# Column-by-column stores from a side tile, and expert biases loaded in their final layout

## The chip, the cores and the metric

The kernel runs on one NeuronCore of one Trainium2 chip. The metric is the device time of one launch in microseconds (us), as the median of several runs. Five engines run their own instruction queues and meet at semaphores: TensorE (PE), VectorE (DVE), ScalarE (ACT), GpSimd (POOL) and SyncE (SP). SP does no arithmetic; it issues most of the transfers.

## The reference

One layer of a hybrid decoder for 256 prompt tokens and 8 sample tokens (264 columns in all). With `D` = 1024:

```
mod = silu(c) @ w_mod + b_mod                       # six rows of 1024: shift, scale, gate, twice
h   = rms_norm(x) * (1 + sc1) + sh1
p   = h @ w_in                                      # q | k | v | p_rw (1792 columns) | gate_a | gate_b
o_a = windowed attention (q, k, v, cache)
o_b, new_wkv = rwkv7_mix(p_rw, prev_row, wkv0, ...)
new_shift = p_rw[:, -1]                             # last token of each sequence, 1792 features
x   = x + gt1 * ((sigmoid(g_a) * (o_a @ w_pa) + sigmoid(g_b) * (o_b @ w_pb)) @ w_o)
y   = moe(rms_norm(x) ...)                          # top 4 of 32 experts
    expert e: u = xe @ w1[e] + b1[e];  clamped SwiGLU;  act @ w2[e] + b2[e]
```

Two pieces matter here. `new_shift` gives the outputs `shift_prompt` (1 row of 1792) and `shift_sample` (8 rows of 1792). `b1` is 32 experts by 2048 biases, 256 KB.

## The kernel before

All activations are kept transposed: features on the 128 partitions, the 264 tokens along the free dimension. The order of the work on every engine is written out by hand; there is no scheduler.

**Weights.** SP walks a list `stream` of 2 MB chunks (`mod` = 512 columns of `w_mod`, `win` = 512 columns of `w_in`, then `pa`, `pb`, `wo`) into six ring slots, and afterwards the experts' `w1` and `w2` in 2 MB pieces. Before each load it waits until the slot's last user is done (`chunk_used`, L332). All these loads go through SP's one queue in this order, so whatever is put between two of them delays the later one. `win` 5 is loaded when `win` 4 has been used, then two copies of the caches (L409, L410), then `win` 6; `mod` 9 follows when the four gate groups of `win` 5 are done.

**TensorE** projects `win` 0 to 4 into `PT` (the 20 blocks of 128 features up to the end of `p_rw`) with modulation chunks between them (L941, L972), then interleaves the gate columns (`gates`, L962) with attention and the recurrence, and needs `mod` 9 at L1143 (`modulation(9)`).

**The shift rows.** `p_rw` of the last token of each sequence is `PTv[:, CR + c, NP - 1:T]`: for each of 14 blocks of 128 features, 9 columns. TensorE transposes the 14 pieces (L1044) in four groups into banks 6 and 7, ScalarE copies each group to the row tile `ssr` (L656), and GpSimd stores `ssr` as rows (L497, L498). These transposes stand between `modulation(8)` and the k and v transposes (L1049, L1053), just ahead of the small decay products (L1059, L1061), whose input ScalarE makes right after its four copies (L659, L660). VectorE turns the decay groups into cumulative sums (L1853, L1856) once a long reciprocal (L1850) is over.

**The expert biases** are loaded as rows (`b1r`, L398), transposed by TensorE in four pieces (L1014), and copied by VectorE into `b1T` (L1808) as 128 x (4 blocks x 128 rows). They are used first in expert 0, at L2242.

What each engine is told to wait for around the change: GpSimd waits for `sh_evac` before the stores, TensorE for `sh_evac` before reusing banks 6 and 7, and SP for `sh_out` before `pb`.

Of the kernel before, what the change touches and what calls it, by code (L numbers as in the profile page):

```python
# [18 lines left out]
P = 128  # L19
D = 1024  # L20
KD = D // P
NP, NS = 256, 8
T = NP + NS
# [4 lines left out]
RW = 1792  # L28
NCH = 20
CQ, CK, CV, CR = 0, 4, 5, 6  # L30
NE, FE, C = 32, 1024, 64
# [91 lines left out]
def build(nc, io):  # L123
    with ExitStack() as ctx:
        sem = Sems(nc, ctx)

        def sb(name, shape, dt=F32):
            return ctx.enter_context(nc.sbuf_tensor(name, shape, dt))


        b1T = sb("b1T", [P, 4, NE * 4])
        modT = sb("modT", [P, 48, 9])
# [70 lines left out]
        OA = view(PT, 0, 4, T)  # L203
        prow, b1r, ext = view(SG, 2048, P), view(SG, 2176, 512), view(SG, 2688, 384)
        crow, csig = view(BM, 0, D), view(BM, 1024, D)
# [32 lines left out]
        SHT = view(XRf, D, KD, 32)  # L238
        wps = view(XM, 0, 4, CH)

        ps = ctx.enter_context(nc.psum_tensor("ps", [P, 8, 512], F32))
# [85 lines left out]
        def a_end(what):  # L327

            i = [name for name, _ in a_order].index(what)
            return sum(n for _, n in a_order[:i + 1])  # L330
# [36 lines left out]
        def _(sp):  # L367
# [7 lines left out]
            for g, (kind, src, j) in enumerate(stream):  # L375
                slot = slots_of[g]
                if g == AFTER_RWKV[0]:
                    sp.wait_ge(sem["carry_evac"], 5)
                    sp.wait_ge(sem["sh_out"], 32)
                    sp.wait_ge(sem["st_kv"], 64)  # L380
                if uses_before(slot, g):
                    last = max(i for i in range(g) if slots_of[i] == slot)
                    sp.wait_ge(*chunk_used(last))
                if kind in ("pa", "pb"):
                    dst = ring[:, slot, :, :].rearrange("p k n -> p (k n)").rearrange("p (k n) -> p k n", n=D)
                    sp.dma_start(dst, io["w_" + kind].rearrange("(k p) n -> p k n", p=P)).then_inc(sem[f"ring{slot}"], 16)
                elif kind == "modA":
                    cols = slice(D, 2 * D) if j < 2 else slice(0, D)
                    sp.dma_start(half_rows(slot), src[:, 4 * (j % 2):4 * (j % 2) + 4, cols]).then_inc(sem[f"ring{slot}"], 16)
                elif (kind, j) == ("win", 0):  # L390
                    sp.dma_start(ring[:, slot, 0:4, :], src[:, 0:4, 0:512]).then_inc(sem["ld_win0"], 16)
                    sp.dma_start(ring[:, slot, 4:8, :], src[:, 4:8, 0:512]).then_inc(sem[f"ring{slot}"], 16)
                else:
                    sp.dma_start(ring[:, slot, :, :], src[:, :, j * 512:j * 512 + 512]).then_inc(sem[f"ring{slot}"], 16)
                if (kind, j) == ("win", 1):
                    sp.dma_start(cst[:, K_FIRST:K_COLS], io["cst"][:, K_FIRST:K_COLS]).then_inc(sem["ld_cst"], 16)
                    sp.dma_start(tab[:, :], io["t5_table"]).then_inc(sem["ld_setup"], 16)
                    sp.dma_start(b1r, io["b1"].rearrange("(r a) f -> r (a f)", a=4)).then_inc(sem["ld_setup"], 16)  # L398
                    sp.dma_start(ssr[0:NS, :], io["state_shift"]).then_inc(sem["ld_setup"], 16)
                    sp.dma_start(LWw[0:64, :], io["rw_w_w2"]).then_inc(sem["ld_lw"], 16)  # L400
                    sp.dma_start(LWw[64:128, :], io["rw_w_a2"]).then_inc(sem["ld_lw"], 16)
                    sp.dma_start(LWg, io["rw_w_g2"]).then_inc(sem["ld_lw"], 16)
                    sp.dma_start(sinkb[:, :], io["sinks"].partition_broadcast(P).rearrange("p a b -> p (a b)")).then_inc(sem["ld_lw"], 16)
                if (kind, j) == ("win", 3):
                    sp.dma_start(kcr, io["cache_k"].rearrange("b j n -> j b n")).then_inc(sem["ld_kc"], 16)
                    sp.wait_ge(*chunk_used(STREAM_AT["win", 0]))
                    sp.dma_start(vcr, io["cache_v"].rearrange("b j n -> j b n")).then_inc(sem["ld_vc"], 16)
                if (kind, j) == ("win", 5):
                    sp.dma_start(io["k_sample"][:, 0:WINDOW - 1, :], io["cache_k"][:, 1:WINDOW, :]).then_inc(sem["st_k"], 16)  # L409
                    sp.dma_start(io["v_sample"][:, 0:WINDOW - 1, :], io["cache_v"][:, 1:WINDOW, :]).then_inc(sem["st_k"], 16)  # L410
# [72 lines left out]
        def _(pool):  # L483
# [11 lines left out]
            pool.dma_start(BM[:, :].rearrange("p (a b) -> p a b", b=2 * P), band).then_inc(sem["ld_bm"], 16)  # L495
            pool.wait_ge(sem["sh_evac"], 4)
            pool.dma_start(io["shift_prompt"], ssr[0:1, :]).then_inc(sem["sh_out"], 16)  # L497
            pool.dma_start(io["shift_sample"], ssr[1:9, :]).then_inc(sem["sh_out"], 16)  # L498
            pool.wait_ge(sem["a_done"], a_end("gate"))
            pool.dma_start(wr, io["w_router"].rearrange("(k p) e -> p k e", p=P)).then_inc(sem["ld_r"], 16)  # L500
            pool.dma_start(brr, io["b_router"]).then_inc(sem["ld_r"], 16)

            pool.wait_ge(sem["kmod_ready"], 1)
            pool.memset(Qz, 0.0).then_inc(sem["pool_part"], 1)
            for hp in range(4):
                chain(pool.tensor_scalar(TM[:, hp, :], r[:, hp, :], par("rw_r_k", hp), None, ALU.mult))
            chain(pool.tensor_tensor(TM, TM, k_mod, ALU.mult))
            pool.wait_ge(sem["decays"], 4)
            pool.wait_ge(sem["sh_t"], 4)

# [50 lines left out]
            pool.wait_ge(sem["ob_ready"], 1)  # L561
            pool.wait_ge(sem["sh_out"], 32)

# [15 lines left out]
        def _(act):  # L579
# [72 lines left out]

            for i in range(4):
                act.wait_ge(sem["sh_t"], i + 1)
                w = min(512, RW - 512 * i)
                act.copy(ssr[0:9, 512 * i:512 * i + w], ps[0:9, 6 + i % 2, 0:w]).then_inc(sem["sh_evac"], 1)  # L656

            act.wait_ge(sem["mixed"], 1)
# [18 lines left out]
            gates(0)  # L677
            act.wait_ge(sem["sh_t"], 4)
            for hp in range(4):
# [192 lines left out]
        def _(pe):  # L872
# [138 lines left out]
            pe.wait_ge(sem["ld_cst"], 16)  # L1011
            pe.wait_ge(sem["ld_setup"], 48)
            for i in range(4):
                last = tr(ps[:, 7, i * P:i * P + P], b1r[:, i::4], ID)  # L1014
            for i in range(14):
# [23 lines left out]
            pe.wait_ge(sem["setup_ready"], 3)  # L1039
            for i in range(4):  # L1040
                if i >= 2:
                    pe.wait_ge(sem["sh_evac"], i - 1)
                for c in range(4 * i, min(4 * i + 4, 14)):
                    last = tr(ps[0:9, 6 + i % 2, (c % 4) * P:(c % 4) * P + P], PTv[:, CR + c, NP - 1:T], ID)  # L1044
                last.then_inc(sem["sh_t"], 1)

            pe.wait_ge(sem["qk_ready"], 1)
# [3 lines left out]
            for kv, (t0, nt) in enumerate(TILES[1:]):  # L1051
                pe.wait_ge(sem["sh_evac"], 3 + kv)
                mm(ps[:, 6 + kv, 0:T], II[64 * kv:64 * kv + 64, :], PTv[64 * kv:64 * kv + 64, CK, :], start=True, stop=True)  # L1053
                tr(ps[0:nt, 6 + kv, T:T + P], PTv[:, CK, t0:t0 + nt], ID).then_inc(sem["kvrow_done"], 1)
# [681 lines left out]
        def _(dve):  # L1736
# [3 lines left out]
            def done(instruction, name, value):  # L1740

                instruction.then_inc(sem[name], 1)
                dve.wait_ge(sem[name], value)
# [60 lines left out]

            dve.wait_ge(sem["ld_setup"], 48)
            v.tensor_copy(tabx[0:NE, :].rearrange("p (b h) -> p b h", h=HQ), tab[:, :].unsqueeze(1).broadcast_to([NE, NS, HQ])).then_inc(sem["tab_ready"], 1)
            dve.wait_ge(sem["setup_t"], 6)
            v.tensor_copy(b1T[:, :, :], ps[:, 7, :].rearrange("p (f r) -> p f r", f=4)).then_inc(sem["setup_ready"], 1)  # L1808
            chain(v.tensor_copy(SS[:, :, :], ps[:, 5, 0:112].rearrange("p (a b) -> p a b", b=NS)))
            v.tensor_copy(brow[:, 0:KEYS], ps[0:NS * HQ, 5, 256:256 + KEYS]).then_inc(sem["brow_ready"], 1)  # L1810
# [181 lines left out]

            dve.wait_ge(sem["sh_out"], 32)
            for n in range(2):
# [243 lines left out]
            def hidden(i, column, hh):  # L2238

                u = ps[:, 2 + hh, :].rearrange("p (f l c) -> p l f c", l=2, f=4)  # L2240
                dve.wait_ge(sem["ut_done"], 2 * i + hh + 1)
                chain(v.tensor_tensor(UG, u[:, 0], b1T[:, :, column(hh)].broadcast_to([P, 4, C]), ALU.add))  # L2242
                v.tensor_scalar(UG, UG, 7.0, None, ALU.min).then_inc(sem["ug_ready"], 1)
                chain(v.tensor_tensor(UL, u[:, 1], b1T[:, :, column(2 + hh)].broadcast_to([P, 4, C]), ALU.add))
                chain(v.tensor_scalar(UL, UL, 7.0, -7.0, ALU.min, ALU.max))
# [57 lines left out]

            dve.wait_ge(sem["a_evac"], a_end("gate2"))
            dve.wait_ge(sem["comb_used"], 1)
            expert(0, 0, first=True)
# [90 lines left out]
```

## Time and profile before

| | us |
|---|---|
| median of 3 runs | 1269.61 (1265.81 to 1270.17) |
| the profiled execution, own time | 1269.29 |
| its span, first to last instruction | 1267.5 |
| PE busy, over the span | 1199.1 (95%) |
| DVE busy | 489.7 (39%) |
| ACT busy | 266.5 (21%) |
| POOL busy | 54.3 (4%) |

The profiled execution's time is 1.8 us longer than its span, for what lies around the first and last instruction. The page has the 16 DMA engines 90% busy or more in nearly every slice from the twelfth on, which is the expert stage; before that they have room, least of it in the first two slices.

### The profile page before, as it was taken

What the parts mean: (1) busy time and instruction counts of PE and PEld (TensorE: products, weight loads), DVE (VectorE), ACT (ScalarE), POOL (GpSimd) and SP (SyncE); (2) the same over time, 40 slices, a digit from 0 to 9 for tenths busy, and PEclk for the clock granted to TensorE, in tenths of its full rate; (3) what the DMA queues carried; (4) which work ended last, traced back from release to release, by engine and by line L of the source; (5) the groups of instructions that cost most, each with busy time, mean ns of one, the idle gap of its engine ahead of it and who ended that gap; (6) DMA issues with size and microseconds to landing.
All of it is one profiled execution on the core that took longest, in us unless ns stands there. A gap on an engine that the chain in (4) does not pass through costs nothing.

```text
span 1267.5 us, 20297 instructions
## 1 busy us (share of the span) xinstructions
PE 1199.1 (95%) x8057; PEld 576.9 (46%) x8057; DVE 489.7 (39%) x1067; ACT 266.5 (21%) x495; POOL 54.3 (4%) x69
## 2 busy tenths in 40 slices
PE   7999999999999999999999999999999999999998
PEld 5887777788743333333333333333333333333333
DVE  3155756555433334433333333333333333333433
ACT  2013651220321112211112112111111122121110
POOL 0010624000000000000000000000000000000000
PEclk9999999999999999999999999999999999999999
DMA  9976331367699999999999999999999999999996
GB/s 369 381 260 250 110 110 70 102 225 304 248 429 423 415 430 431 430 430 431 432 432 431 432 431 431 431 432 432 431 431 431 431 431 431 432 432 431 430 430 271
DMA packets 57906, 467.22 MB, mean 369 GB/s; under 512 B 5245, under 2 KB 8577, under 8 KB 32618
## 3 DMA queue, kind: packets, MB, share of 16 engines
q1 hardware_dynamic: 55098, 460.55, 86.9%
q0 software_dynamic: 1664, 5.20, 1.5%
q8 instruction: 44, 0.72, 0.2%
q10 hardware_dynamic: 1088, 0.66, 0.2%
q14 instruction: 12, 0.10, 0.0%
HBM read 463.91 MB, written 5.09 MB: 370 GB/s over the span
## 4 chain that ended last, share of the span: by engine, by line
PE 67%; DMA 27%; ACT 2%; DVE 2%; issue 1%; SPq 0%; DVEq 0%
DMA ring<-in_w 27%; PE ps L1557 21%; PE ps L1582 12%; PE ps L972 5%; PE ps L1483 3%; PE ps L962 3%; PE ps L1506 3%; PE ps L1431 2%; PE ps L1399 2%; PE ps L1568 2%; PE ps L980 1%; PE ps L1490 1%; ACT PH L843 1%; PE ps L941 1%; PE ps L917 1%
## 5 line engine op out<-in xcount | busy, mean ns | idle before, releaser
L1557 PE MATMUL ps<-ring,PH 128*64 128x512 f32 x1472 | 327.5, 594 | 23.8 <-DMA ring<-in_w 23.7
L2231 DVE TENSOR_TENSOR SQ<-ps,SQ 128x512 f32<-128x512 f32 x124 | 77.0, 683 | 411.9 <-PE ps L1506 411.8
L1557 PEld LDWEIGHTS ps<-ring,PH 128*64 128x64 f32 x1472 | 103.6, 137 | 239.6 <-issue 188.8
L1582 PE MATMUL ps<-ring,PH 128*64 128x512 f32 x736 | 163.0, 595 | 0.0
L838 ACT COPY PH<-ps 128x512 f32<-128x512 f32 x62 | 33.3, 589 | 576.6 <-PE ps L1557 576.6
L1557 PE MATMUL ps<-arena,PH 128*64 128x512 f32 x504 | 112.2, 594 | 7.5 <-DMA arena<-in_w 7.5
L1582 PEld LDWEIGHTS ps<-ring,PH 128*64 128x64 f32 x736 | 50.8, 137 | 95.8 <-issue 95.8
L1557 PEld LDWEIGHTS ps<-arena,PH 128*64 128x64 f32 x504 | 35.3, 137 | 82.5 <-issue 65.6
L972 PE MATMUL ps<-PH,ring 128*128 128x264 f32 x304 | 69.3, 388 | 0.2 <-issue 0.2
L2224 DVE TENSOR_TENSOR PH<-ps,XR 128x512 f32<-128x512 f32 x31 | 21.4, 692 | 108.4 <-PE ps L1582 108.4
L972 PEld LDWEIGHTS ps<-PH,ring 128*128 128x128 f32 x304 | 57.3, 190 | 10.7 <-issue 1.1
L1483 PE MATMUL ps<-XR,PH 128*64 128x512 f32 x256 | 62.0, 605 | 0.2 <-DVE PH L2169 0.2
L1506 PE MATMUL ps<-PH 64*128 64x512 f32 x248 | 61.6, 614 | 0.0
L962 PE MATMUL ps<-PH,ring 128*128 128x264 f32 x208 | 57.8, 421 | 0.1
L1582 PE MATMUL ps<-arena,PH 128*64 128x512 f32 x248 | 55.0, 595 | 0.0
L962 PEld LDWEIGHTS ps<-PH,ring 128*128 128x128 f32 x208 | 39.2, 200 | 9.0 <-issue 1.7
L838 ACT ACT_TABLE_LOAD x31 | 39.8, 1283 | 0.9 <-issue 0.4
L841 ACT ACT_TABLE_LOAD x31 | 39.8, 1283 | 0.5
L1506 PEld LDWEIGHTS ps<-PH 64*128 64x128 f32 x248 | 21.3, 185 | 39.8 <-issue 39.8
L1568 PEld LDWEIGHTS ps<-cst,PH 128*128 128x128 f32 x256 | 27.4, 141 | 25.9 <-ACT PH L838 24.3
L576 POOL TENSOR_TENSOR SQ<-PH,SQ 128x256 f32<-128x256 f32 x2 | 1.4, 717 | 825.8 <-ACT PH L863 825.8
L1568 PE MATMUL ps<-cst,PH 128*128 128x128 f32 x256 | 35.2, 280 | 0.7 <-ACT PH L838 0.7
(485 smaller groups left out, 1173.8 us busy)
## 6 DMA issues: line engine op xcount, KB each, us to landing
ring<-in_w SPq DMA_DIRECT2D x143, 2048.0 KB, 31.5
arena<-in_w SPq DMA_DIRECT2D x46, 2048.0 KB, 31.6
ring<-in_w_mod SPq DMA_DIRECT2D x12, 2048.0 KB, 14.5
ring<-in_w_in SPq DMA_DIRECT2D x8, 2048.0 KB, 12.1
ring<-in_w_o SPq DMA_DIRECT2D x2, 2048.0 KB, 10.7
ring<-in_w_in SPq DMA_DIRECT2D x2, 1024.0 KB, 17.3
ring<-in_w_pa SPq DMA_DIRECT2D x1, 2048.0 KB, 8.1
ring<-in_w_pb SPq DMA_DIRECT2D x1, 2048.0 KB, 9.0
```

The source lines that it names most:

```text
L838: act.copy(UR[:, h, :].rearrange("p (f r) -> p f r", f=4), ps[:, 2 + h, :].rearrange("p (r f) -> p f r", f=4)).then_inc(sem["ur_evac"], 1)
L841: act.activation(US_, UG, ACT.Sigmoid, scale=1.702).then_inc(sem["us_ready"], 1)
L962: last = mm(ps[:, GATE_BANK[b], 0:T], w[:, k, s * P:s * P + P], HT[:, k, :], start=(k == 0), stop=(k == KD - 1))
L972: last = mm(bank[:, 0:T], w[:, k, s * P:s * P + P], HT[:, k, :], start=(k == 0), stop=(k == KD - 1))
L1399: last = mm(ps[:, k % 4, 0:T], w[:, i, k * P:k * P + P], (OA, OT)[q][:, i, :], start=(i == 0), stop=(i == 3))
L1431: last = mm(ps[:, 4 + k % 2, 0:T], w[:, i, (k % 4) * P:(k % 4) * P + P], HT[:, i, :], start=(i == 0), stop=(i == KD - 1))
L1483: last = mm(ps[64 * s:64 * s + 64, 0, :], OH[:, n, :], XR[:, n, s * 512:s * 512 + 512], start=(n == 0), stop=(n == 1))
L1506: last = mm(ps[:, banks[m][s], :], GT[64 * s:64 * s + 64, m * P:m * P + P], YS[64 * s:64 * s + 64, :], start=start, stop=True)
L1557: last = mm(ps[64 * lin:64 * lin + 64, 2 + hh, :], XG[:, k % 4, k // 4, :], slot_row(slot, c, k % 2, lin * FE + hh * 512), start=(k == 0), ...
L1568: last = tr(ps[:, 2 + hh, f * P:f * P + P], UR[:, hh, f * P:f * P + P], ID)
L1582: last = mm(ps[64 * hh:64 * hh + 64, 4, :], AC[:, f, :], slot_row(slot, c, f % 4, hh * 512), start=(f == 0), stop=(f == NF - 1))
L2231: v.tensor_tensor(acc, ps[:, banks[p // 2][p % 2], :], acc, ALU.add).then_inc(sem["comb_used"], 1)
```

## The change

The 14 transposes, the four ScalarE copies and the GpSimd row stores go. In their place GpSimd copies the 9 x 14 columns into a side tile `SHC` (126 elements per partition), which lies in `b1T`'s memory, and SP stores it with nine DMAs, one for each of the 9 rows: each moves 14 elements of each of the 128 partitions to addresses that are not neighbours, 1792 single elements of 4 bytes. They stand in SP's queue right behind the load of `win` 6.

The row tile `b1r`, its load, the four transposes and the VectorE copy go. In their place SP loads `b1` into `b1T` directly, behind `win` 8 and after the nine stores have landed. `b1T` is now laid out as 128 rows x 4, so that each partition takes 4 neighbouring floats (16 bytes) of each of 128 rows: 16,384 pieces.

```diff
-        b1T = sb("b1T", [P, 4, NE * 4])
+        b1T = sb("b1T", [P, NE * 4, 4])
...
+        SHC = view(b1T[:, :, :].rearrange("p a b -> p (a b)"), 0, 14, 1 + NS)
...
@@ SyncE
                 if g == AFTER_RWKV[0]:
                     sp.wait_ge(sem["carry_evac"], 5)
-                    sp.wait_ge(sem["sh_out"], 32)
                     sp.wait_ge(sem["st_kv"], 64)
...
-                    sp.dma_start(b1r, io["b1"].rearrange("(r a) f -> r (a f)", a=4)).then_inc(sem["ld_setup"], 16)
...
+                if (kind, j) == ("win", 6):
+                    sp.wait_ge(sem["sh_copied"], 1)
+                    for b in range(1 + NS):
+                        row = io["shift_sample"][b - 1:b, :] if b else io["shift_prompt"]
+                        sp.dma_start(row.rearrange("o (c p) -> p c o", p=P), SHC[:, :, b:b + 1],
+                                     allow_slow_non_contiguous=True).then_inc(sem["sh_out"], 16)
+                if (kind, j) == ("win", 8):
+                    sp.wait_ge(sem["sh_out"], 16 + 16 * NS)
+                    sp.dma_start(b1T[:, :, :], io["b1"].rearrange("(r x) y -> r (x y)", x=4).rearrange("r (p f) -> p r f", f=4)).then_inc(sem["ld_b1"], 16)
...
@@ GpSimd
-            pool.wait_ge(sem["sh_evac"], 4)
-            pool.dma_start(io["shift_prompt"], ssr[0:1, :]).then_inc(sem["sh_out"], 16)
-            pool.dma_start(io["shift_sample"], ssr[1:9, :]).then_inc(sem["sh_out"], 16)
+            pool.wait_ge(sem["a_evac"], a_end("win4"))
+            pool.tensor_copy(SHC[:, :, :], PTv[:, CR:NCH, NP - 1:T]).then_inc(sem["sh_copied"], 1)
...
             pool.wait_ge(sem["kmod_ready"], 1)
+            pool.wait_ge(sem["sh_copied"], 1)
...
             pool.wait_ge(sem["decays"], 4)
-            pool.wait_ge(sem["sh_t"], 4)
...
             pool.wait_ge(sem["ob_ready"], 1)
-            pool.wait_ge(sem["sh_out"], 32)
+            pool.wait_ge(sem["sh_out"], 16 + 16 * NS)
...
@@ ScalarE
-            for i in range(4):
-                act.wait_ge(sem["sh_t"], i + 1)
-                w = min(512, RW - 512 * i)
-                act.copy(ssr[0:9, 512 * i:512 * i + w], ps[0:9, 6 + i % 2, 0:w]).then_inc(sem["sh_evac"], 1)
...
-            act.wait_ge(sem["sh_t"], 4)
+            act.wait_ge(sem["sh_copied"], 1)
             for hp in range(4):
                 act.copy(GG[:, hp, :], group()).then_inc(sem["a_evac"], 1)
...
@@ TensorE
-            pe.wait_ge(sem["ld_setup"], 48)
-            for i in range(4):
-                last = tr(ps[:, 7, i * P:i * P + P], b1r[:, i::4], ID)
+            pe.wait_ge(sem["ld_setup"], 32)
...
-            for i in range(4):
-                if i >= 2:
-                    pe.wait_ge(sem["sh_evac"], i - 1)
-                for c in range(4 * i, min(4 * i + 4, 14)):
-                    last = tr(ps[0:9, 6 + i % 2, (c % 4) * P:(c % 4) * P + P], PTv[:, CR + c, NP - 1:T], ID)
-                last.then_inc(sem["sh_t"], 1)
-
...
             for kv, (t0, nt) in enumerate(TILES[1:]):
-                pe.wait_ge(sem["sh_evac"], 3 + kv)
...
@@ VectorE
-            v.tensor_copy(b1T[:, :, :], ps[:, 7, :].rearrange("p (f r) -> p f r", f=4)).then_inc(sem["setup_ready"], 1)
-            chain(v.tensor_copy(SS[:, :, :], ps[:, 5, 0:112].rearrange("p (a b) -> p a b", b=NS)))
+            done(v.tensor_copy(SS[:, :, :], ps[:, 5, 0:112].rearrange("p (a b) -> p a b", b=NS)), "setup_ready", 3)
...
-            dve.wait_ge(sem["sh_out"], 32)
             for n in range(2):
...
-                chain(v.tensor_tensor(UG, u[:, 0], b1T[:, :, column(hh)].broadcast_to([P, 4, C]), ALU.add))
+                chain(v.tensor_tensor(UG, u[:, 0], b1T[:, column(hh), :].rearrange("p r f -> p f r").broadcast_to([P, 4, C]), ALU.add))
...
             dve.wait_ge(sem["a_evac"], a_end("gate2"))
+            dve.wait_ge(sem["ld_b1"], 16)
             dve.wait_ge(sem["comb_used"], 1)
```

On SyncE, from the two cache copies to `pb`. Here `out_k_sample` and `out_v_sample` are the cache copies, `in_w_in` behind them is `win` 6, the next `in_w_mod` is `mod` 9, and `in_w_pa` and `in_w_pb` are `pa` and `pb`. Before:

```order
L410 DMA out_v_sample<-in_cache_v 8x16256
L394 DMA ring<-in_w_in 128x8x512 [waits a_done]
L394 DMA ring<-in_w_mod 128x8x512 [waits f_done]
L394 DMA ring<-in_w_in 128x8x512 [waits a_done]
L394 DMA ring<-in_w_in 128x8x512 [waits f_done]
L386 DMA ring<-in_w_pa 128x4x1024 [waits f_done]
L386 DMA ring<-in_w_pb 128x4x1024 [waits st_kv,a_done,sh_out,carry_evac]
```

And now, with `in_b` as the name of `b1`:

```order
L418 DMA out_v_sample<-in_cache_v 8x16256
L394 DMA ring<-in_w_in 128x8x512 [waits a_done]
L411 DMA out_shift_prompt<-b1T 128x14x1 [waits sh_copied]
L411 DMA out_shift_sample<-b1T 128x14x1 x8
L394 DMA ring<-in_w_mod 128x8x512 [waits f_done]
L394 DMA ring<-in_w_in 128x8x512 [waits a_done]
L394 DMA ring<-in_w_in 128x8x512 [waits f_done]
L415 DMA b1T<-in_b 128x128x4 [waits sh_out]
L386 DMA ring<-in_w_pa 128x4x1024 [waits f_done]
L386 DMA ring<-in_w_pb 128x4x1024 [waits a_done,st_kv,carry_evac]
```

Nine stores now stand ahead of `mod` 9, and the bias load, with its wait for them, ahead of `pa`.

On TensorE, from `modulation(8)` to the first decay product. Before:

```order
L941 MATMUL ps<-ring,cT 32x128 x31
L1044 MATMUL ps<-cst,PH 9x128 [waits setup_ready,ms_ready]
L1044 MATMUL ps<-cst,PH 9x128 x7
L1044 MATMUL ps<-cst,PH 9x128 [waits sh_evac]
L1044 MATMUL ps<-cst,PH 9x128 x3
L1044 MATMUL ps<-cst,PH 9x128 [waits sh_evac]
L1044 MATMUL ps<-cst,PH 9x128
L1049 MATMUL ps<-cst,PH 128x128 [waits qk_ready]
L1049 MATMUL ps<-cst,PH 128x128
L1049 MATMUL ps<-cst,PH 8x128
L1053 MATMUL ps<-PH,cst 128x264 [waits sh_evac]
```

And now, where L1042 is the former L1049, L1045 and L1046 the former L1053 and L1054, and L1051 the former L1059:

```order
L943 MATMUL ps<-ring,cT 32x128 x31
L1042 MATMUL ps<-cst,PH 128x128 [waits qk_ready,setup_ready,ms_ready]
L1042 MATMUL ps<-cst,PH 128x128
L1042 MATMUL ps<-cst,PH 8x128
L1045 MATMUL ps<-PH,cst 128x264
L1046 MATMUL ps<-cst,PH 128x128
L1045 MATMUL ps<-PH,cst 128x264
L1046 MATMUL ps<-cst,PH 8x128
L1051 MATMUL ps<-arena,ring 128x264 [waits a_evac,lora_in,ld_lw]
```

The 14 transposes and the waits for ScalarE's copies are gone; nothing else moved.

## Rows read from the trace of the kernel before

**Rows 1.** Stretch: us, PE, PEld, DVE, ACT, POOL busy, granted clock, DMA share, GB/s.
```profile
350.00:1260.00 910.00, 867.38 (x4178) 308.06 (x4177) 313.11 (x727) 169.36 (x258) 3.30 (x4) 1.00 1.00 427
```

**Rows 2.** Who TensorE waited for, 380 to 1250 us (total, times, longest).
```profile
PE ps L1557 <- DMA ring<-in_w: 23.7, 26, 1.3
```

**Rows 3.** The chain that ended last (start, duration, what).
```profile
62.47 0.48 PE ps L1014 x4
...
119.45 0.55 PE ps L1044 x4
...
121.92 0.71 PE ps L1053 x2
...
124.27 1.91 PE ps L1059 x5
...
145.79 0.52 PE ps L1094 x4
```

**Rows 4.** ScalarE in order of time: start, duration, instruction, idle time before.
```profile
115.71 0.38 ACT L618 COPY PH<-ps 128x264 f32<-128x264 f32 x1 [3.18 <-PE ps L972]
...
119.52 0.27 ACT L627 COPY RS<-ps 128x128 f32<-128x128 f32 x1 [1.52 <-PE ps L941]
...
122.15 1.28 ACT L659 ACT_TABLE_LOAD   x1
...
144.31 1.28 ACT L694 ACTIVATE ring<-ring,st 128x128 f32<-128x128 f32 x4 [0.31 <-DVE st L1918]
```

**Rows 5.** VectorE in order of time, same columns.
```profile
120.23 6.75 DVE L1850 RECIPROCAL SQ<-SQ 128x1056 f32<-128x1056 f32 x1
...
128.13 0.71 DVE L1853 TENSOR_SCALAR ring<-ring 128x1056 f32<-128x1056 f32 x1 [1.14 <-ACT ring L662]
```

**Rows 6.** GpSimd in order of time: a copy of 129 elements in a partition.
```profile
66.02 1.06 POOL L488 COPY arena<-brow 8x129 f32<-8x129 f32 x1
```

**Rows 7.** SyncE's queue in order of time: `win` 6, `mod` 9, `win` 7 and 8, `pa`.
```profile
119.51 0.37 SPq L394 DMA_DIRECT2D ring<-in_w_in  x1
151.74 0.37 SPq L394 DMA_DIRECT2D ring<-in_w_mod  x1
175.18 21.85 SPq L394 DMA_DIRECT2D ring<-in_w_in  x2
...
244.22 0.37 SPq L386 DMA_DIRECT2D ring<-in_w_pa  x1
```

**Rows 8.** Us from issue to landing: `win` 6, `mod` 9, `pa`.
```profile
ring<-in_w_in SPq DMA_DIRECT2D x1, 2048.0 KB, 15.3
...
ring<-in_w_mod SPq DMA_DIRECT2D x1, 2048.0 KB, 7.7
...
ring<-in_w_pa SPq DMA_DIRECT2D x1, 2048.0 KB, 8.1
```

**Rows 9.** TensorE in order of time: `modulation(9)`, the products with `pa` and `pb`.
```profile
173.17 1.95 PE L941 MATMUL ps<-ring,cT 128*32 128x128 f32 x64
277.04 3.16 PE L1399 MATMUL ps<-PH,ring 128*128 128x264 f32 x13 [0.48 <-ACT arena L620]
```

**Rows 10.** Queue shares: packets, MB, share of 16 engines; in 265:271, 69.5:72, 118:122.
```profile
q10 hardware_dynamic: 540, 0.13, 9.9%
...
q1 hardware_dynamic: 1598, 0.83, 113.2%
...
q1 hardware_dynamic: 773, 1.58, 103.5%
```

**Rows 11.** TensorE and DMA by stretch: busy, granted clock, DMA share, GB/s.
```profile
125.00:126.00 1.00, 1.00 (x5) 0.50 1.42 593
...
133.00:151.70 18.70, 18.25 (x104) 1.00 0.03 7
...
180.00:260.00 80.00, 76.31 (x1902) 0.94 0.24 80
```

**Rows 12.** Tile `b1T`: its users in the expert stage.
```profile
L2242 DVE TENSOR_TENSOR PH<-ps,b1T x64: 411/414/426, 370.2 to 1253.3; 128x256 f32<-128x256 f32 x64
```

More of the change, by code:

```diff
@@ L203, in build @@
         OA = view(PT, 0, 4, T)
-        prow, b1r, ext = view(SG, 2048, P), view(SG, 2176, 512), view(SG, 2688, 384)
+        prow, ext = view(SG, 2048, P), view(SG, 2688, 384)
         crow, csig = view(BM, 0, D), view(BM, 1024, D)
@@ L1803, in _ @@
             done(last, "setup_ready", 2)
-            dve.wait_ge(sem["ld_setup"], 48)
+            dve.wait_ge(sem["ld_setup"], 32)
             v.tensor_copy(tabx[0:NE, :].rearrange("p (b h) -> p b h", h=HQ), tab[:, :].unsqueeze(1).broadcast_to([NE, NS, HQ])).then_inc(sem["tab_ready"], 1)
             dve.wait_ge(sem["setup_t"], 6)
-            v.tensor_copy(b1T[:, :, :], ps[:, 7, :].rearrange("p (f r) -> p f r", f=4)).then_inc(sem["setup_ready"], 1)
-            chain(v.tensor_copy(SS[:, :, :], ps[:, 5, 0:112].rearrange("p (a b) -> p a b", b=NS)))
+            done(v.tensor_copy(SS[:, :, :], ps[:, 5, 0:112].rearrange("p (a b) -> p a b", b=NS)), "setup_ready", 3)
             v.tensor_copy(brow[:, 0:KEYS], ps[0:NS * HQ, 5, 256:256 + KEYS]).then_inc(sem["brow_ready"], 1)
@@ L2241, in hidden @@
                 dve.wait_ge(sem["ut_done"], 2 * i + hh + 1)
-                chain(v.tensor_tensor(UG, u[:, 0], b1T[:, :, column(hh)].broadcast_to([P, 4, C]), ALU.add))
+                chain(v.tensor_tensor(UG, u[:, 0], b1T[:, column(hh), :].rearrange("p r f -> p f r").broadcast_to([P, 4, C]), ALU.add))
                 v.tensor_scalar(UG, UG, 7.0, None, ALU.min).then_inc(sem["ug_ready"], 1)
-                chain(v.tensor_tensor(UL, u[:, 1], b1T[:, :, column(2 + hh)].broadcast_to([P, 4, C]), ALU.add))
+                chain(v.tensor_tensor(UL, u[:, 1], b1T[:, column(2 + hh), :].rearrange("p r f -> p f r").broadcast_to([P, 4, C]), ALU.add))
                 chain(v.tensor_scalar(UL, UL, 7.0, -7.0, ALU.min, ALU.max))
```

## The prediction

> **What bounds the kernel now.** I read the stretches first, then the waits of TensorE, then the chain. From 350 to 1260 us the DMA share is 1.00 at 427 GB/s and TensorE is busy 867 of 910 us [rows 1]; its largest wait there is for weights, 26 times, 23.7 us in all [rows 2]. So the expert stage runs at the pace of its weights, and the change takes nothing out of it. It can only start earlier or later: its first loads are released by TensorE's progress, so a us won or lost on the chain before 277 us is a us of the total. That chain runs through TensorE, and both places that the change clears stand on it: the transposes of `b1r` at 62.47 and those of the shift rows at 119.45 [rows 3].
>
> **What goes, and what it is worth.** The four `b1r` transposes are 0.48 us of the chain [rows 3], and nothing else was late there: the next instruction is TensorE's own. Gain 0.48. VectorE's copy into `b1T` goes too; it is off the chain, as GpSimd, which it held up, waits for TensorE later anyway. I give it nothing.
>
> The shift transposes and the copies between them last from 119.45 to 121.92, 2.47 us [rows 3]. Not all of it comes back. ScalarE can start its table load after its copy at 119.52 + 0.27 = 119.8 instead of 122.15 [rows 4], so the first decay product starts some 2.3 us earlier than 124.27 [rows 3]. But the decay goes to VectorE, which is in a reciprocal from 120.23 to 126.98 and now waits only 1.14 us after it for ScalarE, until 128.13 [rows 5]. The reciprocal hangs on `win` 4, not on the shift rows. So VectorE comes late next, and of 2.47 us 1.14 count; the rest turns into waiting on TensorE. From there the chain goes through VectorE's sums, the first softmax and ScalarE's last product, which ends at 144.31 + 1.28 = 145.59, 0.2 us before TensorE takes it at 145.79 [rows 3, 4]: both sides move by the 1.14, and neither eats it. Lower bound 0 (something else due at the same moment), upper bound 2.47; I take 1.14, since the wait is measured. Sum: 0.48 + 1.14 = 1.62 us.
>
> **What is added on GpSimd.** One copy of 126 elements per partition. A copy of 129 took 1.06 us [rows 6], and 0 is the other end; I take 1.06. GpSimd is idle before it, and ScalarE has written its input, the last block of `win` 4, by 115.71 + 0.38 = 116.1 [rows 4], so it ends near 117.2, before SyncE has issued `win` 6 at 119.51 [rows 7]. The wait for it on SyncE costs nothing, nor does the one on ScalarE, much later.
>
> **What is added on the queue.** This is the term that decides. Nine stores of 1792 single elements are 16,128 pieces, 1008 for each of the 16 DMA engines if they share them evenly, all in SyncE's queue between `win` 6 and `mod` 9. `win` 6 lands at 119.51 + 15.3 = 134.8 [rows 7, 8]; I let the pieces start only then. From 133 to 151.7 the DMA share is 0.03 [rows 11], so this is a free stretch. `mod` 9 is queued behind: issued at 151.74, 7.7 us to landing, first used at 173.17 [rows 7 to 9], or 171.6 with the gain. So the pieces must be done by 171.6 - 7.7 = 163.9, in 29.1 us: 28.9 ns a piece on each engine. Beyond it TensorE stands still in `modulation(9)`, and everything behind it in its queue (the sample attention, the recurrence, `pa`, `pb`) with it: stall = 1.008 x piece cost - 29.1.
>
> No row shows a 4-byte piece of data. The nearest: 256-byte writes to HBM (with their semaphore writes) while other loads ran, 540 packets for 9.9% of 16 engines over 6 us, so 17.6 ns each; 512-byte reads, 1598 packets for 113.2% over 2.5 us, 28.3 ns; 2 KB reads, 773 packets for 103.5% over 4 us, 85.7 ns [rows 10]. The lower end is 0, the far upper end 85.7. I take 17.6: it is the smallest, it writes to HBM, and it is the row in which the bytes count least. That makes 17.7 us, done at 152.5, 11.4 us inside the limit: cost 0. At 28.3 it is 28.5 us, still just hidden; at 85.7 it is 86.4 us and a stall of 57.3.
>
> The Trainium skill, "DMA: Bandwidth & Descriptors", section Rules for kernel authors, speaks against the form of this store: a last dimension with strides becomes one descriptor per element. That agrees with the count above, and the sum does not need it. The same page, section Specifications, says that below 512 bytes a transfer is done as read-modify-write. The 256-byte row shows no such doubling against the 512-byte one (17.6 against 28.3 ns); if the rule bites only on smaller pieces, it is the first rival below.
>
> **The bias load.** 16,384 pieces of 16 bytes, 1024 per engine, queued behind `win` 8, which SyncE has issued by 175.18 + 21.85 = 197.03 [rows 7]; with a landing like that of `pa` (8.1 [rows 8]) they start at 205.1. At 17.6 ns they take 18.0 us, to 223.1, before `pa` is even issued at 244.22 [rows 7]. `pa` and `pb` are needed at 277.04 [rows 9]; two landings of 8.1 before that is 260.8, so the limit is 55.7 us, 54 ns a piece. The wait for the nine stores is over by then in the same case. The biases are used first at 370.2 [rows 12]. Cost 0. Lost with it is only a 256 KB load early on. In the expert stage the bias add reads four neighbouring floats instead of four 512 bytes apart; it takes 414 ns, 64 times [rows 12], on an engine busy 313 of 910 us [rows 1]: nothing either way.
>
> **Sum.** The profiled execution took 1269.29 us (span 1267.5 and 1.8 around it), 0.3 under the median of 1269.61. 1269.29 - 1.62 = 1267.7; with the 0.3, 1268.0. The change gains 0.13%, which is less than can be told here: about 0.5%, 6.3 us, separates a result from no change.
>
> **Rivals.**
> - *A 4-byte write costs twice the 256-byte one*, 35.2 ns. The pieces take 35.5 us, the stall is 6.4 us, and the time 1268.0 + 6.4 = 1274.4. For it: pieces this small are not in the trace, and neighbouring partitions write neighbouring 4-byte places. Against it: no sign of it at 256 bytes. Still no measurable change. Chance 0.10.
> - *The stores outlast their gap* (slower). Place: `mod` 9 behind the nine stores; it decides from 28.9 ns a piece, and is measurable from 36.7 ns (stall 7.9 us). As its price I take 49 ns, an estimate, the geometric middle of 28.3 and 85.7: 49.4 us, stall 20.3, 1288.3. For it: all the slack is 29 us, in one queue. Against it: the cost falls with size down to the smallest row. Chance 0.20.
> - *The bias load holds up `pa` and `pb`*, from 54 ns on, while the stores are cheap: at 85.7 ns it takes 87.8 us, 32 over its limit, 1300. Reads of 16 bytes into the chip have less against them than writes. Chance 0.02.
> - *The clock moves* (faster). TensorE is at half clock (1.2 GHz) at 125 us, after short products and waits for ScalarE, and its mean clock is 0.94 from 180 to 260 us, which is 9.6 us at half clock, or 4.8 us of full work lost [rows 11]. The stretch at 125 lies under VectorE's wait and gives nothing back. If a shifted program lost all of that, 1268.0 - 4.8 = 1263.2, 6.4 us faster, 0.50%. The engine does the same work before them as now, so I don't expect it. Chance 0.05.
>
> **How the numbers follow.** The forecast, hidden stores and 1.62 us of gain, has 0.63 with 1265 to 1271 (gain 0 to 2.95, and one stretch of low clock more or less). Faster: 0.05. Same: 0.63 + 0.10 = 0.73. Slower: 0.20 + 0.02 = 0.22. The range goes from 1263, the clock's case, to 1288, the price of the slower rival, whose upper half stays outside.
>
> **What would show it.** Right: the nine stores in the profile land before about 155 us, `mod` 9 about 7.7 us after its issue, TensorE has no DMA wait at `modulation(9)`, the first decay product starts near 121.5, VectorE goes from the reciprocal into the decay without a wait, and `modulation(9)` comes 1.6 us earlier, at 171.6. Wrong: a wait of TensorE for the ring at `modulation(9)`, or at `pa`, or a DMA share that stays up between 135 and 170.

## The result

| | before | after |
|---|---|---|
| median, us | 1268.54 (1265.81 to 1270.17, 4 runs) | 1313.45 (1307.9 to 1323.78, 4 runs) |
| ratio, with 95% interval | | 1.0362 (1.0333 to 1.0391) |
| profiled execution, own time / span | 1269.29 / 1267.5 | 1323.78 / 1322.0 |
| PE / DVE / ACT / POOL busy | 1199.1 / 489.7 / 266.5 / 54.3 | 1202.9 / 488.9 / 264.4 / 52.9 |

The change makes the kernel 3.6% slower, 45 us at the medians. The forecast was 1268.0 with a range to 1288: both were wrong. The profiled execution of after is its longest run, 10.3 us above its own median. So places and waits are read from it, and the price of the change from the medians; how long the wait was in the other three executions, no trace shows.

The arithmetic engines do the same work as before, and their busy times hardly move; nearly all of the 45 us is waiting.

### The profile page after: what moved, and what is told of

It reads as the page before. It is cut to its first block, busy times and chain, and to the rows that moved or that the text cites. A ratio compares the mean times of both kernels' runs of the same rounds, so it can differ in the third digit from the quotient of the medians.

```text
span 1322.0 us, 20265 instructions
## 1 busy us (share of the span) xinstructions
PE 1202.9 (91%) x8039; PEld 580.7 (44%) x8039; DVE 488.9 (37%) x1066; ACT 264.4 (20%) x491; POOL 52.9 (4%) x68
## 4 chain that ended last, share of the span: by engine, by line
PE 63%; DMA 28%; SPq 6%; ACT 1%; issue 1%; DVE 1%; DVEq 0%
DMA ring<-in_w 26%; PE ps L1549 20%; PE ps L1574 11%; SPq L411 5%; PE ps L974 5%; PE ps L1475 3%; PE ps L1498 3%; PE ps L964 2%; PE ps L1423 2%; PE ps L1391 2%; DMA ring<-in_w_mod 2%; PE ps L1560 2%; PE ps L982 1%; PE ps L1482 1%; PE ps L943 1%
## 5 line engine op out<-in xcount | busy, mean ns | idle before, releaser
L974 PEld LDWEIGHTS ps<-PH,ring 128*128 128x128 f32 x304 | 57.3, 190 | 10.7 <-issue 1.1
L943 PE MATMUL ps<-ring,cT 128*32 128x128 f32 x384 | 13.4, 299 | 43.8 <-DMA ring<-in_w_mod 43.8
```

Of the source, the lines that this page charges most:

```text
L943: last = mm(bank[32 * s:32 * s + 32, 0:P], cT[:, k, :], w[:, k, s * P:s * P + P], start=(k == 0), stop=(k == KD - 1))
L974: last = mm(bank[:, 0:T], w[:, k, s * P:s * P + P], HT[:, k, :], start=(k == 0), stop=(k == KD - 1))
```

## The profile after

The page, its slices of 33 us each (busy tenths of the DMA engines, then the granted clock):

```profile
DMA  9976996515769999999999999999999999999996
PEclk9999966798999999999999999999999999999999
```

SyncE's queue in order of time (start, duration, what), which answers to [rows 7]:

```profile
119.25 0.37 SPq L394 DMA_DIRECT2D ring<-in_w_in  x1
119.67 2.72 SPq L411 DMA_DIRECT2D out_shift_prompt<-b1T  x1
122.43 68.34 SPq L411 DMA_DIRECT2D out_shift_sample<-b1T  x8
190.81 3.01 SPq L394 DMA_DIRECT2D ring<-in_w_mod  x1
219.55 22.60 SPq L394 DMA_DIRECT2D ring<-in_w_in  x2
242.19 0.58 SPq L415 DMA_DIRECT2D b1T<-in_b  x1
```

SyncE is held for 68 us while it issues eight stores, and `mod` 9 behind them is issued at 190.81, 39 us later than before. Then it takes 25.0 us to land instead of 7.7 [rows 8]:

```profile
ring<-in_w_mod SPq DMA_DIRECT2D x1, 2048.0 KB, 25.0
```

The pieces ahead of it explain some 9 of the 25 us. The packets of all queues from 115 to 130 us and from 115 to 200 us, where those under 512 bytes are nearly all pieces of the stores, and `mod` 9's queue from 198 to 208 us (packets, MB, share of 16 engines):

```profile
DMA packets 2779, 4.78 MB, mean 319 GB/s; under 512 B 944, under 2 KB 944, under 8 KB 2762
...
DMA packets 18814, 6.80 MB, mean 80 GB/s; under 512 B 16480, under 2 KB 16496, under 8 KB 18666
...
q1 hardware_dynamic: 326, 0.48, 96.2%
```

The first 920 pieces move between 126 and 130 us, beside `win` 6, and the last before 200. After that only 2 KB packets of `mod` 9 are left, and from 200 to 206 us one of them takes some 560 ns (164 packets for 95.4%) where it took 86 in [rows 10]. Why they crawl when no piece is under way any more, no run shows.

TensorE in order of time at `modulation(9)`, which answers to the first of [rows 9]. In brackets are the idle time before it and what ended that:

```profile
215.84 3.64 PE L943 MATMUL ps<-ring,cT 128*32 128x128 f32 x64 [43.84 <-DMA ring<-in_w_mod]
```

The chain that ended last (start, duration, what), here from the stores on. Before, it ran through TensorE, VectorE and ScalarE in this place, and through no transfer:

```profile
122.43 16.66 SPq L411
...
190.81 24.98 DMA ring<-in_w_mod
215.84 3.64 PE ps L943 x64
...
251.81 2.05 issue
...
257.70 2.85 issue
...
300.74 2.77 issue
```

By stretch (us, busy time of PE, PEld, DVE, ACT, POOL, granted clock, DMA share, GB/s), beside [rows 11] and [rows 1]:

```profile
133.00:151.70 18.70, 17.71 (x97) 13.79 (x99) 11.97 (x25) 9.97 (x36) 13.28 (x9) 0.91 0.89 20
174.00:277.00 103.00, 55.51 (x1175) 46.66 (x1177) 34.51 (x52) 13.01 (x31) 15.62 (x7) 0.70 0.62 72
396.00:1306.00 910.00, 866.09 (x4216) 307.69 (x4217) 313.14 (x746) 173.36 (x264) 3.30 (x4) 1.00 1.01 430
```

The DMA engines were 3% busy from 133 to 151.7 us before [rows 11]. Now they are 89% busy, and almost nothing goes through them. The expert stage, here shifted by 46 us, has not changed.

The queue in two short stretches (packets, MB, share of 16 engines), for the price of one piece. During the stores, 142 to 145 us:

```profile
q1 hardware_dynamic: 830, 0.00, 126.5%
```

During the bias load, 248 to 260 us:

```profile
q1 hardware_dynamic: 16582, 0.60, 114.5%
```

The first gives 1.265 x 16 x 3 us / 830 = 73 ns a piece on an engine, where I had taken 17.6. It is not the same in every stretch: from 145 to 155 us it is 57 ns, from 155 to 165 us 98. The second gives 1.145 x 16 x 12 us / 16,582 = 13.3 ns. Both kinds of piece are tiny, and they differ by a factor of five.

**Where the profiled 54.5 us went.** `modulation(9)` starts 42.7 us later (215.84 against 173.17 [rows 9]). It then takes 1.7 us longer, at 3.64 against 1.95. From its end to the products with `pa` and `pb` it is 111.6 us against 101.9, 9.7 more; of these, 4.3 are `issue` pauses (7.67 in sum against 3.36 before, see below). The rest, 5.4 us, I put down to the clock: in this part the granted clock is 0.89 against 0.95 before, and TensorE is busy for 102.7 us against 97.5 with the same matmuls, 5.3 more. The three sum to 54.1. At the medians the loss is 44.9, of which the wait less the gain, 43.8 - 1.5, is 42.3.

## The experiments

Three questions were asked. Is it the nine stores? What makes their pieces so slow? And is anything else lost? Medians are in us, each against the kernel before on the same chip. A ratio comes with its 95% interval.

**1. No stores.** After, without the nine stores (`shift_prompt` and `shift_sample` aren't written).

```diff
-                    for b in range(1 + NS):
-                        row = io["shift_sample"][b - 1:b, :] if b else io["shift_prompt"]
-                        sp.dma_start(row.rearrange("o (c p) -> p c o", p=P), SHC[:, :, b:b + 1], ...
```

> The changed kernel with the nine column stores left out (shift_prompt and shift_sample are not written; the copy into the side tile stays). If the stores alone make the loss, modulation(9) has no DMA wait and starts near 171.6 us, and the time is 1267 (my term of 1.62 us for what the change removes) to 1269. If the bias load has a part in the loss (in the changed kernel TensorE loses some 6 us more than before between 250 and 264 us, while the 16-byte pieces are loaded), it stays: 1272 to 1275.

Measured: 1271.07, ratio 1.0027 (1.0008 to 1.0045). SyncE's queue and the pauses on the chain:

```profile
173.71 20.69 SPq L394 DMA_DIRECT2D ring<-in_w_in  x2
194.45 0.58 SPq L410 DMA_DIRECT2D b1T<-in_b  x1
```

```profile
203.66 2.21 issue
...
209.84 2.77 issue
...
252.17 1.51 issue
```

The loss is gone but for 1.6 us, so it is the stores. `win` 7, which `modulation(9)` releases, is issued 1.47 us earlier than before (175.18 [rows 7]), so the gain on the chain is real. Yet the kernel is not faster: TensorE pauses for 6.49 us at `issue` where before it paused for 3.36 (1.15 at 208.66, 0.55 at 213.09 and 1.66 at 251.82). The 3.1 us more, less the forecast gain of 1.6, is 1.5; the medians differ by 1.6.

**2. The bias part alone**, on the kernel before, with the load behind `win` 8.

```diff
-        b1T = sb("b1T", [P, 4, NE * 4])
+        b1T = sb("b1T", [P, NE * 4, 4])
...
+                if (kind, j) == ("win", 8):
+                    sp.dma_start(b1T[:, :, :], io["b1"].rearrange("(r x) y -> r (x y)", x=4).rearrange("r (p f) -> p r f", f=4)).then_inc(...)
```

> The kernel before with only the bias part of the change: b1 loaded in its final layout behind win 8, the four transposes, the copy and the row load gone; the shift rows go the old way. If the bias part is worth what I said (0.48 us, load hidden): 1268.1, a tie with the kernel before. If the load of 16,384 pieces holds up TensorE's instructions: 1272 to 1275, as in the run without stores.

Measured: 1273.92, ratio 1.004 (1.0022 to 1.0057). The waits of TensorE (us in total, times, longest) and the pieces of the chain:

```profile
PE ps L1277 <- issue: 6.4, 2, 4.1
```

```profile
205.46 2.00 issue
...
210.00 4.15 issue
...
257.98 1.61 issue
```

The 16-byte load costs 4 to 5 us, though nothing waits for its data. The two larger pauses begin in the some 10 us (202 to 212) in which its pieces are under way, and all three sum to 7.8 us against 3.4. In this stretch TensorE runs some 30 matmuls of 64x64 in 0.7 to 1.1 us, so new instructions have to come in quickly. They come by DMA as well. The queues from 200 to 215 us of before:

```profile
q8 instruction: 4, 0.07, 1.6%
```

The same from 202 to 215 us of this kernel:

```profile
q1 hardware_dynamic: 16592, 0.62, 105.0%
q8 instruction: 2, 0.03, 1.8%
```

A packet of instructions took 0.016 x 16 x 15 / 4 = 0.96 us before, and takes 0.018 x 16 x 13 / 2 = 1.87 us beside the bias pieces. These are few packets, but other runs agree: 1.9 to 2.2 us beside the bias pieces in after and in experiments 1, 3, 4, 8, 9 and 10, and 0.96 to 1.1 without them in the same place in experiments 5, 6, 11 and 12. I read this as the likely cause of the pauses, though a pause of 4.15 us is longer than such a packet; experiments 5 and 6 move the load away from it.

**3. Into the chip's own memory.** The same nine DMAs with the same 4-byte pieces, but their target is unused columns of `b1T`.

```diff
-                        sp.dma_start(row.rearrange("o (c p) -> p c o", p=P), SHC[:, :, b:b + 1],
+                        sp.dma_start(SHD[:, b, :, 0:1], SHC[:, :, b:b + 1],
```

> The changed kernel with the same nine DMAs of 1792 4-byte pieces, but written to free columns of b1T in SBUF in place of the outputs in HBM (outputs not written). Theory A (the write of 4 bytes into HBM is what costs, some 65 ns a piece on each engine): the nine are done in some 10 to 20 us, no wait at modulation(9), 1267 to 1270. Theory B (any 4-byte piece costs that, by its descriptor or its read from SBUF): SyncE is again held for some 70 us and the time is about 1313.

Measured: 1273.34, ratio 1.0038 (1.0023 to 1.0053), no DMA wait at `modulation(9)`. SyncE:

```profile
119.45 20.78 SPq L412 DMA_DIRECT2D b1T<-b1T  x9
```

and the queue from 140 to 145 us:

```profile
q1 hardware_dynamic: 3667, 0.01, 32.6%
```

That is 7 ns a piece, and the nine stores hold SyncE for 20.8 us instead of 71.1 (119.67 to 190.77). Neither the number of pieces nor their size makes them slow; the target does.

**4. Spread over 512 bytes.** To HBM, but into a scratch tensor in which each piece has 512 bytes to itself.

```diff
+        far_d = nc.dram_tensor("far", [1 + NS, P, 14, 128], F32, kind="Internal")
...
-                        sp.dma_start(row.rearrange("o (c p) -> p c o", p=P), SHC[:, :, b:b + 1],
+                        sp.dma_start(far_d.ap()[b, :, :, 0:1], SHC[:, :, b:b + 1],
```

> The changed kernel with the nine stores going to a scratch tensor in HBM in which every 4-byte piece has 512 bytes of its own (outputs not written). Theory A1 (pieces of neighbouring partitions, from different DMA engines, fall into the same few bytes of HBM and wait for each other): the spread makes it quick, no wait at modulation(9), 1267 to 1272. Theory A2 (a partial write into HBM costs its engine some 65 ns wherever it goes): nothing changes, the wait at modulation(9) is about 44 us and the time about 1313.

Measured: 1272.93, ratio 1.0028 (1.0007 to 1.0049), no DMA wait. SyncE and the queue from 140 to 145 us:

```profile
120.44 28.98 SPq L411 DMA_DIRECT2D far<-b1T  x9
152.63 0.38 SPq L395 DMA_DIRECT2D ring<-in_w_mod  x1
```

```profile
q1 hardware_dynamic: 2954, 0.01, 134.7%
```

At 1.347 x 16 x 5 us / 2954 = 36 ns of packet time they just fit, since the packets of an engine overlap: SyncE has issued all nine after 29 us, and `mod` 9 goes out at once. A write of 4 bytes to HBM is therefore not slow by itself. What differs from after is how near to each other the pieces land. Because of the overlap, packet time is not the pace: here 36 ns of packet time go with 27 ns from piece to piece (5 us x 16 / 2954), and in experiment 3 7 ns go with 22. The time that SyncE is held tells the pace better.

**5 and 6. The bias load earlier.** Experiment 1 and experiment 2, each with the load moved from behind `win` 8 to behind `win` 6. There TensorE is in `win` products, long ones, and the queue is free.

```diff
-                if (kind, j) == ("win", 8):
+                if (kind, j) == ("win", 6):
                     sp.dma_start(b1T[:, :, :], ...
```

> As the run without stores (outputs shift_prompt and shift_sample not written), with the bias load moved from behind win 8 to behind win 6, where TensorE runs long products. Theory I (the 16,384 small reads slow the fetch of TensorE's instructions just where it runs through some 300 short ones; 2.2 and 2.8 us of issue waits at 204 and 210 us): the waits there fall back to some 1.7 us in all, and the time is the forecast of the prediction, 1267.8. Theory II (those waits come from the place of the instructions in memory, which the change shifted, and not from the bias load): they stay, 1271.

> The kernel before with only the bias part of the change, the load placed behind win 6. Theory I: 1269, a tie with the kernel before or 0.5 us less, the issue waits at 205 and 210 us (2.0 and 4.15 in the run with the load behind win 8) gone down to about 1.7 in all. Theory II: they stay, 1273.

Measured: without stores 1267.0, ratio 1.0002 (0.9977 to 1.0027); the bias part alone 1266.95, ratio 0.9992 (0.9975 to 1.0009). The chain of the latter:

```profile
206.52 0.86 issue
...
249.10 1.61 issue
```

The 3 to 5 us are gone in both, and the large pauses with them. For the bias part alone the intervals stand clear of each other (experiment 2 from 1.0022 on, this one up to 1.0009); with the whole change less the stores they overlap, and the pauses in the trace are what tells them apart. This shows that the place of the load decides; that it does so through the instruction packets is read from the packet times, and no run isolates it. Both medians lie 2.0 us under that of the kernel before, 1268.98, but both intervals take in no change at all, so the forecast gain of 1.6 us (0.5 for the bias part) is neither confirmed nor denied by the times.

**7. Dense, and each partition by itself.** To a scratch tensor in which the 14 pieces of a partition are neighbours and partitions are 56 bytes apart. If only pieces of different partitions hindered each other, this would be quick.

```diff
+        far_d = nc.dram_tensor("far", [1 + NS, P, 14, 1], F32, kind="Internal")
...
+                        sp.dma_start(far_d.ap()[b, :, :, :], SHC[:, :, b:b + 1],
```

> The changed kernel with the nine stores into a scratch tensor in which the 14 pieces of one partition are neighbours and partitions follow each other 56 bytes apart (outputs not written): the same 4-byte pieces and as dense, but neighbours in memory mostly come one after the other from one DMA engine. If only pieces from different engines hinder each other: about as fast as the spread stores, no wait at modulation(9), 1273. If any partial write waits for the one before it in the same few bytes: a wait of 20 us or more there.

Measured: 1338.34, ratio 1.0549 (1.0517 to 1.0581), the slowest of all. SyncE, and TensorE's wait:

```profile
119.58 85.32 SPq L411 DMA_DIRECT2D far<-b1T  x9
```

```profile
PE ps L943 <- DMA ring<-in_w_mod: 64.5, 1, 64.5
```

So what I expected fell: pieces side by side from one partition are no better than those from several, but worse. It also shows that it was not the scratch tensor as such that made experiment 4 quick.

**8 and 9. 64 and 32 bytes apart**, in the order of the output. The diff is of 8; 9 has 8 in place of the 16.

```diff
+        far_d = nc.dram_tensor("far", [1 + NS, 14, P, 16], F32, kind="Internal")
...
+                        sp.dma_start(far_d.ap()[b, :, :, 0:1].rearrange("c p w -> p c w"), SHC[:, :, b:b + 1],
```

> The changed kernel with the order of the outputs (14 blocks, in each the 128 partitions) but 64 bytes from piece to piece in a scratch tensor (outputs not written). If the pieces hinder each other only inside the same 64 bytes: as the 512-byte spread, the nine issued in some 29 us, 1273. If the unit is larger, or all engines working in the same few KB is what counts: SyncE is held for 40 to 70 us and the time lies between 1280 and 1313.

> The order of the outputs again, now 32 bytes from piece to piece in a scratch tensor (outputs not written). If the unit in which 4-byte writes hinder each other is 32 bytes: as the 64-byte spread, nine DMAs issued in some 30 us, about 1273. If it is 64 bytes, two pieces share one: SyncE is held for 40 us or more, with a wait at modulation(9).

Measured: 1273.51, ratio 1.0034 (1.001 to 1.0058), and 1272.81, ratio 1.0038 (1.0016 to 1.006), both without a DMA wait. SyncE with 32 bytes, and its queue from 140 to 145 us:

```profile
120.52 27.70 SPq L411 DMA_DIRECT2D far<-b1T  x9
```

```profile
q1 hardware_dynamic: 4473, 0.02, 116.2%
```

That is 21 ns a piece (64 bytes: 24, from 116.8% for 3940). Already at 32 bytes the stores are as quick as at 512, in the same order in which they are slow at 4. So 32 bytes are enough to keep pieces out of each other's way; 8 and 16 bytes were not tried. The 0.3% that stays is that of experiment 1, the bias load: its pauses are there again, 7.2 us on the chain with 32 bytes and 6.9 with 64, against 3.4 before.

**10. Five of the nine rows** (the other four aren't written).

```diff
-                    for b in range(1 + NS):
+                    for b in range(5):
```

> The changed kernel with five of the nine column stores (four rows of shift_sample are not written). From the changed kernel's trace a piece costs about 73 ns per engine, so 5 x 112 x 73 = 41 us, 12 over the 29.1 us that the prediction found before modulation(9): a wait there of about 12 us in place of 43.8 and a time near 1272 + 12 = 1284. If the loss were a fixed one of having such stores at all, the wait would be 30 us or more.

Measured: 1290.66, ratio 1.0167 (1.0139 to 1.0195). TensorE's wait:

```profile
PE ps L943 <- DMA ring<-in_w_mod: 19.0, 1, 19.0
```

The wait grows with the number of pieces, so it is no fixed cost of having such stores. But the formula asks for 19.0 + 29.1 = 48.1 us for 560 pieces an engine, which is 86 ns a piece, not 73, and the 12 us that I expected were too few. The trace shows why. The pieces go from 126 to 169 us, 43 us or 77 ns each, much as in after. Then `mod` 9 lands only at 190.7, 22 us behind the last piece, where the formula has 7.7. So the piece does not cost more with fewer rows: a slow landing of the load behind comes on top, in after as here.

**11. Neighbours kept apart in time.** The whole change in 72 DMAs, each with every eighth partition, so that pieces of one DMA land 32 bytes apart; the bias load behind `mod` 9.

```diff
-                    for b in range(1 + NS):
-                        row = ...
-                        sp.dma_start(row.rearrange("o (c p) -> p c o", p=P), SHC[:, :, b:b + 1], ...
+                    for i in range(8):
+                        for b in range(1 + NS):
+                            row = ...
+                            sp.dma_start(row.rearrange("o (c p) -> p c o", p=P)[i::8], SHC[i::8, :, b:b + 1], ...
```

> The whole change with other stores: each row in eight DMAs, each of every eighth partition, so that pieces in flight together lie 32 bytes apart, and the eight sweeps over all rows follow each other (72 DMAs in place of 9; all outputs written); the bias load behind mod 9. If writes close together are the cause: the stores are done in 25 to 35 us (SyncE needs some 0.45 us for each of the 72), no wait or a few us at modulation(9), 1267 to 1272, a tie with the kernel before. If not: 1310 or more.

Measured: 1285.84, ratio 1.0122 (1.0099 to 1.0146), 28 us faster than after and still 16 slower than before. SyncE from the third round of nine on, the wait, and the queue from 140 to 145 us:

```profile
140.85 0.61 SPq L412 DMA_DIRECT2D out_shift_prompt<-b1T  x1
141.50 5.15 SPq L412 DMA_DIRECT2D out_shift_sample<-b1T  x8
...
178.53 0.60 SPq L394 DMA_DIRECT2D ring<-in_w_mod  x1
```

```profile
PE ps L944 <- DMA ring<-in_w_mod: 15.1, 1, 15.1
```

```profile
q1 hardware_dynamic: 1920, 0.01, 19.1%
```

The same 4-byte pieces to the same addresses now take 0.191 x 16 x 5 / 1920 = 8 ns. Slower feeding is not the reason: SyncE hands out all 1008 for an engine in 57.9 us, one every 57 ns, and after got through one only every 71 ns (71.1 us). This confirms the cause in the kernel itself. What I missed is SyncE: an issue holds it for some 0.6 us or more, 72 of them from 120.64 to 178.53, and `mod` 9 is late again, this time behind instructions, not behind pieces.

**12. Two halves.** As 11, with four rounds behind `win` 6 and four behind `mod` 9, and the bias load behind `win` 7.

```diff
-                if (kind, j) == ("win", 6):
+                if (kind, j) in (("win", 6), ("mod", 9)):
...
+                    for i in range(4) if kind == "win" else range(4, 8):
```

> As the run with every eighth partition (all outputs written), but only 36 of the 72 DMAs stay behind win 6 and 36 go behind mod 9; the bias load goes behind win 7. In the run before SyncE itself needed 58 us for the 72 (the plain ones 0.61 us each), so mod 9 was issued at 178.5 and TensorE waited 15.1 us. If SyncE's issue time was all that was left: 26 us each, hidden in the two gaps, mod 9 issued at 151.7, no wait at modulation(9), win 7 some 3 us late but needed 10 us after that, and 1267 to 1270, a tie with the kernel before. If the writes themselves still cost: a wait of 10 us or more.

Measured: 1270.03, ratio 1.0015 (1.0001 to 1.0028). There is no DMA wait at `modulation(9)`. SyncE (this profile runs some 3.5 us late from its start on) and the largest pause:

```profile
149.60 5.16 SPq L412 DMA_DIRECT2D out_shift_sample<-b1T  x8
155.45 0.38 SPq L394 DMA_DIRECT2D ring<-in_w_mod  x1
```

```profile
PE ps L1332 <- issue: 1.5, 1, 1.5
```

The whole change, with these two repairs, takes 43 us less than after and is within 0.5% of before. No kernel here beats the one before by more than its interval.

## Why the prediction was wrong

Step by step, in the order of the prediction:

- **What bounds the kernel: right.** A us lost before 277 us was a us of the total. The products with `pa` and `pb` came 54.1 us later in the profile, and the end 54.5. The expert stage kept its pace.
- **Gain on the chain, 0.48 + 1.14: right in sum.** With the stores away it was 1.47 of 1.62 us; no run has the two parts by themselves. VectorE goes from the reciprocal to the decay without a wait, as foretold:

```profile
120.07 6.75 DVE L1841 RECIPROCAL SQ<-SQ 128x1056 f32<-128x1056 f32 x1
126.86 0.71 DVE L1844 TENSOR_SCALAR ring<-ring 128x1056 f32<-128x1056 f32 x1
```

- **GpSimd's copy at 1.06: too dear, without effect.** It took 0.28 us:

```profile
115.89 0.28 POOL L505 COPY b1T<-PH 128x126 f32<-128x126 f32 x1 [17.57 <-ACT PH L625]
```

- **"I take 17.6": the step that failed.** The price of a piece was mis-sized: 73 ns were measured. The place held (`mod` 9 behind nine stores), and so did the form of the loss, a wait of TensorE for `mod` 9. I ordered the rows of the trace by bytes and went to the smallest [rows 10]. But the bytes were not what counted: at 4 bytes a piece costs 7 ns into the chip's own memory, 21 to 36 into HBM from 32 bytes apart on, and 73 side by side (experiments 3, 4, 8, 9). No row showed neighbouring writes from several places, and I had named that very point ("neighbouring partitions write neighbouring 4-byte places") as being for a rival, at 35 ns.
- **The rest of that term: two errors that nearly cancel.** With 73.2 ns the formula gives 1.008 x 73.2 - 29.1 = 44.7, where 43.8 were measured, but that is partly luck. "I let the pieces start only then", at 134.8: they started at 126, beside `win` 6, and were all done by 200, 74 us for 1008 pieces an engine, while the formula with 73 ns ends them near 209. "7.7 us to landing": `mod` 9 landed some 16 us behind the last piece. Experiment 10, with its 86 ns by the same formula, shows that the two do not always cancel. SyncE's own time in the issues was put at nothing. Even with quick pieces it is 20.8 us for nine (experiment 3), which ended before `mod` 9 was due; with 72 it decided (experiment 11).
- **The rivals.** The slower one had the place and the mechanism, with a chance of 0.20 and a price of 49 ns. That price was a middle between two rows of another kind. The far end that I had kept, 85.7 ns and a stall of 57.3, held the truth, and the range left it out. The Trainium skill, "DMA: Bandwidth & Descriptors", section Specifications, has a read-modify-write below 512 bytes. A rule by size alone does not tell these runs apart: 4 bytes at 512, 64 and 32 bytes of distance fit into the gap, and at 4 bytes of distance they don't. Whether the hindrance is a read-modify-write of a smaller unit that two writers share, no run here can show.
- **"The bias load: cost 0": wrong by 3 to 5 us.** The pieces were even cheaper than I took (13.3 ns against 17.6), and `pa` and `pb` had no wait. It costs by a way that I didn't think of, TensorE's pauses at `issue` beside it (experiments 1, 2, 5, 6); what links the two is only read from packet times. By itself this would have left the forecast inside its range.
- **The clock.** It moved the other way than in the rival. The granted clock was 0.70 over 174 to 277 us against 0.95 before, with 43.8 us of standing still in it, and `modulation(9)` behind it ran at 1.2 GHz, 3.64 us for 1.95. A long stall costs more than its length, here up to 7 us in the profiled execution (1.7 in `modulation(9)` and the 5.4 above).

## What to carry to other kernels

Price a scattered store by where its pieces land, not by their size: here 4-byte pieces side by side in HBM held the issuing queue 2.5 to 3 times as long as the same pieces 32 bytes or more apart, and a queue that holds them holds every load behind them. Before pieces are put into a "free" stretch, work out the price per piece from which the stretch is too short; where no row shows such pieces, and a factor of two decides, the far end belongs into the range. A load that nobody waits for can still slow an engine that has short instructions, probably because instructions come by DMA too; moving the load to a stretch of long instructions removed the loss.

## What the runs showed of the hardware

- Packet time of a 4-byte piece on a DMA engine: 73 ns into HBM at 4 bytes of distance (57 to 98 by stretch), 21 to 36 at 32 to 512 bytes, 7 into on-chip memory. A 16-byte piece read from HBM took 13.3 ns.
- SyncE was held by the same nine stores for 71.1 us at 4 bytes of distance, 27.5 to 29.0 at 32 to 512 bytes, 20.8 into on-chip memory, and 85.3 where the pieces of one partition lie side by side, the slowest.
- SyncE can be held inside an issue: 68.3 us for eight stores of 1792 slow pieces, against 0.61 us for most stores of an eighth of that size (experiment 11). I read this as a queue that is full; no run isolates it.
- A 2 MB load behind the slow pieces took 16 to 22 us from the last piece to its landing (after, experiment 10), against 7.7 us in all before.
- Beside a load of 16-byte pieces, a packet of instructions took 1.87 us instead of 0.96, and TensorE paused for up to 4.15 us.
